# Writing the first PEER head's gates into a zeroed DRAM matrix with plain indirect DMAs instead of adding indirect DMAs

## The reference, cut to what matters

```python
def peer(h, w_q, sub_keys, u_tab, v_tab):      # shortened
    q = (xc @ w_q).reshape(ch, PEER_HEADS, 2, half)
    s = jnp.einsum('thpd,hpnd->thpn', q, sub_keys)
    v1, i1 = lax.top_k(s[:, :, 0], PEER_TOPK)
    v2, i2 = lax.top_k(s[:, :, 1], PEER_TOPK)
    ...
    e = i1_picked * N_KEYS + i2_picked          # one of 128*128 experts
    g = jax.nn.softmax(vals, axis=-1)
    act = jax.nn.gelu(jnp.einsum('td,thkd->thk', xc, u_tab[e])) * g
    return jnp.einsum('thk,thkd->td', act, v_tab[e])
```

## Time and profile before

| what | us |
|---|---|
| median of 3 runs | 3285.22 |
| lowest, highest | 3275.11, 3285.28 |
| profiled execution, its span | 3278.9 |
| TensorE matmul busy | 3197.4 |
| VectorE busy | 2016.1 |
| GpSimd busy | 1912.5 |
| ScalarE busy | 1237.3 |

### The profile page before, as it was taken

One profiled execution on the slowest core, in us unless ns is written; L12 is line 12 of the kernel. 1 busy time (PEld: TensorE's weight loads), 2 busy tenths in 40 slices (PEclk: granted clock), 3 DMA queues, 4 the chain that ended last, 5 costly groups with the idle time before them and its releaser, 6 DMA issues. The chain is left out here.

```text
span 3278.9 us, 47570 instructions
## 1 busy us (share of the span) xinstructions
PE 3197.4 (98%) x15034; PEld 2600.4 (79%) x15034; DVE 2016.1 (61%) x4043; ACT 1237.3 (38%) x1838; POOL 1912.5 (58%) x1318
## 2 busy tenths in 40 slices
PE   8889999999999999999899899999999999999999
PEld 7578888888887788887766678888888887888887
DVE  4667575752224888888646656676732225888888
ACT  3544233334433333333425633333332223333333
POOL 0005888888888756555000007888888886655554
PEclk9999999999999999999999999999999999999999
DMA  5925565666667999999319115655566668999998
GB/s 191 337 74 133 119 149 117 133 148 144 144 146 232 370 350 348 352 345 333 124 34 320 41 65 127 139 135 128 125 145 145 145 145 274 355 351 351 355 347 303
DMA packets 399381, 681.95 MB, mean 208 GB/s; under 512 B 145472, under 2 KB 239680, under 8 KB 399040
## 3 DMA queue, kind: packets, MB, share of 16 engines
q1 hardware_dynamic: 218944, 520.95, 47.1%
q0 software_dynamic: 155648, 134.82, 20.1%
q10 hardware_dynamic: 24704, 25.17, 2.3%
HBM read 560.85 MB, written 119.94 MB: 208 GB/s over the span
## 5 line engine op out<-in xcount | busy, mean ns | idle before, releaser
L1783 POOL DMA_INDIRECT gate_matrix<-pe_misc x768 | 1285.8, 1674 | 734.9 <-DVE pe_misc L2354 501.5
L2052 PE MATMUL psum<-split,ex_ah 128*128 128x512 f32 x2976 | 921.7, 391 | 10.1 <-DVE ex_al L2497 8.1
L427 PE MATMUL psum<-up_hhi,up_hi 128*128 128x512 f32 x2048 | 798.1, 390 | 0.0
L427 PE MATMUL psum<-up_hlo,up_hi 128*128 128x512 f32 x2048 | 796.8, 389 | 0.0
L427 PE MATMUL psum<-up_hhi,up_lo 128*128 128x512 f32 x2048 | 796.8, 389 | 0.0
L418 DVE TENSOR_TENSOR up_lo<-up_raw,up_hi 128x1024 fp32r<-128x1024 f32 x256 | 313.7, 1226 | 757.9 <-ACT up_hi L414 693.6
L2052 PEld LDWEIGHTS psum<-split,ex_ah 128*128 128x128 f32 x2976 | 555.3, 188 | 139.7 <-DVE ex_al L2497 20.8
L2052 PE MATMUL psum<-split,ex_al 128*128 128x512 f32 x1488 | 579.2, 389 | 0.0
L1793 POOL DMA_INDIRECT ex_gv<-in_v,ga_at x256 | 274.0, 1070 | 329.2 <-DVE x_sb L2447 306.6
L427 PEld LDWEIGHTS psum<-up_hhi,up_lo 128*128 128x128 f32 x2048 | 384.4, 188 | 79.8
L427 PEld LDWEIGHTS psum<-up_hlo,up_hi 128*128 128x128 f32 x2048 | 384.5, 188 | 79.3
(11 more groups left out here) (374 smaller groups left out, 3164.6 us busy)
## 6 DMA issues: line engine op xcount, KB each, us to landing
up_raw<-in_uT SPq DMA_DIRECT2D x256, 512.0 KB
ro_wq<-in_v SPq DMA_DIRECT2D x256, 512.0 KB
gelu<-up_z SPq DMA_DIRECT2D x256, 256.0 KB
pe_misc<-gelu SPq DMA_DIRECT2D x256, 192.0 KB
ex_gm<-gate_matrix SPq DMA_DIRECT2D x124, 384.0 KB
gate_matrix<-ga_at ACTq DMA_DIRECT2D x8, 3072.0 KB, 13.6
gate_matrix<-ga_at SPq DMA_DIRECT2D x8, 3072.0 KB, 23.2
ro_wq<-in_peer_wq SPq DMA_DIRECT2D x32, 512.0 KB
```

What stands on the lines that cost most here:

```text
L427: last = pe.matmul(self.ps[:, a, :], w[:, a, dc, :], h[:, dc, :], start=(dc == 0 and m == 0), stop=(dc == DC - 1 and m == 2))
L1783: pool.indirect_dma_start(place, bass.IndirectOffsetOnAxis(ap=to[:, j:j + 1], axis=0), gates[:, j:j + 1], None, compute_op=ALU.add).then_i ...
L2052: last = pe.matmul(psy[:, o, :], w[:, par, a, toks], v[:, par, a, cols], start=False, stop=(final and m == 2))
```

## The change

The helper `scatter` gives each indirect DMA the operation to do at its destination. It was an addition for all heads. Now it is a plain write (bypass) for head 0 and an addition for heads 1 to 7.

```diff
@@ def scatter(self, pool, gmat, to, gates, h, t)
             pool.wait_ge(done.sem, done.base + 16 * TOPK * h)
         for j in range(h * HW + t * TOPK, h * HW + (t + 1) * TOPK):
             pool.indirect_dma_start(place, bass.IndirectOffsetOnAxis(ap=to[:, j:j + 1], axis=0), gates[:, j:j + 1], None,
-                                    compute_op=ALU.add).then_inc(done.sem, 16)
+                                    compute_op=ALU.add if h > 0 else ALU.bypass).then_inc(done.sem, 16)
```

## The result

| kernel | runs | median us | lowest to highest |
|---|---|---|---|
| before, beside it | 4 | 3281.64 | 3275.11 to 3285.28 |
| changed | 4 | 3365.65 | 3360.25 to 3368.66 |

The ratio is 1.0254, 95% interval 1.0237 to 1.0272. The forecast was 3284.5 us in a range that ended at 3293. The profiled execution has a span of 3361.8 us, 82.9 more than before, with the same 47570 instructions.

What follows compares the result with a forecast made beforehand. PE was taken to bound the kernel. Head 0's 2 x 29 us saved on POOL became waiting or ended unneeded, 0 to -1 us on PE; with the run-to-profile difference carried over, 3284.5 us, range 3272 to 3293.

Steps and rivals of the forecast that it cites:

- What bounds the kernel now: Whole kernel: PE bounds, busy 98% of the span; it loses only 0.34 and 1.12 us around the two change-overs.
- Part 1, POOL's time: Head 0's 48 scatters per layer: slot 1.4 us instead of 1.997, so POOL finishes head 0 29 us earlier.
- "wrong if": Failure signs: first 48 slots over 2.05 us, no POOL wait before the 49th, or change-over PE time moving over 2 us.
- "PE full in the U stretches": Sign expected in the changed trace: PE without holes during the U products, and the change-overs as before.
- Part 2, what is late next: Head 1's start: POOL waits for DVE's gates, so only 1.5 us are won per layer and 27 us become waiting.
- Part 3, the end: Change-overs after the last scatters: these end 1.5 us earlier in each layer, and PE gains zero.
- SP's wait at L1945: Layer 0's end, SP waiting for the last scatter's completion: about 1.9 instead of 3.4 us.
- Part 4, DMA load: DMA engines during head 0: cheaper plain writes for 96 of 768 scatters, where PE waits for nothing; worth 0.
- A (same price on POOL): Head 0's scatters: a plain write costs POOL the same as an add; 3285.2 us, chance 0.26.
- B (slower): Head 0: plain scatters held up beside DVE make POOL's end pass PE's slack; 3303 to 3405 us, chance 0.07.
- C (faster): Head 1's gates or change-overs: the 29 us reach PE, faster by more than 0.3%; chance 0.05.

Runs made afterwards that it cites:

- chip A: Chip of the first follow-up group; against the kernel before: head 1 plain 0.9990, all heads plain 0.9994, head 0 plain with pauses 1.0512.
- the paced kernel: Changed kernel (head 0 plain) with a GpSimd memset and drain after each head 0 scatter; 3448.62 us, 1.0512 of the kernel before.
- chips B to E: Chips of the four later follow-up groups; the unedited changed kernel against the kernel before: 1.0284, 1.0295, 1.0266 and 1.0284.
- with gathers: Head 0's 48 scatters of each layer replaced by plain 4-byte gathers from the same places; 3376.46 us, 1.0289 of the kernel before.
- chip C: Chip of the third group; against the kernel before: changed kernel 1.0295, head 1 plain 1.0273, all heads plain 1.2182, head 0 plain with pauses 1.0513.

## Why the prediction was wrong, step by step

**What bounds the kernel now**: right. PE does, without a hole; so whatever holds up PE is paid in full, and 82.1 of 82.9 us arise in head 0 (44.0 and 38.1).

**Part 1, POOL's time**: right in kind, and too dear. A slot of 1.4 us was forecast, 1.27 measured, since the plain scatter takes 0.97 us almost always (0.94 and stretching came to 1.1 in the forecast); in the mean of the 48 it is 1.33. POOL is done at 333.8 (forecast 337). None of the three "wrong if" came true: the slots were 1.33 us in the mean and not 2.05, the wait before the 49th was there (76.19 us, where 25 to 30 were forecast), and the change-overs kept their PE time. What went wrong lay outside that list; of the signs forecast, "PE full in the U stretches" is the one that failed. The Trainium skill, "SBUF — State Buffer", section "A bandwidth-pool intuition that's wrong (but worth ruling out)", with its 3100 ns beside VectorE, isn't borne out for these DMAs: with all 768 plain the longest took 2.08 us.

**Part 2, what is late next**: right about the mechanism and right about its size on chip A, where the 49th started at 365.35 (forecast 364.5). It failed on the sentence "DVE's time for head 1 isn't set by POOL: the selection is interleaved with the splits of U tiles, which keep PE's pace, and PE has no holes to give". Nothing on DVE or ACT waits for POOL indeed. But POOL's faster issue made the holes in PE, and through PE's late signals DVE's time for head 1 was set by POOL after all.

**Part 3, the end**: right; that an earlier end of the scatters is worth nothing is shown by POOL's 225.7 us of waiting in the all-plain kernel on chip A, at a ratio of 0.9994. SP's wait at L1945 was forecast at 1.9 us and stayed 3.4, since nothing became earlier.

**Part 4, DMA load**: this step failed. It weighed only the load of the DMA engines ("cheaper... PE waits for nothing... Worth 0") and was right on that: queue 0 moves 10752 packets fewer (144896), 112 for each plain scatter. What it never asked is what POOL's pace does to others. The mean slot fell from 2.00 to 1.33 us, and that term, costed at nothing, measured +83 us (84.0 by the medians). The long add had held GpSimd's issue to one DMA in 2.00 us, and that turned out to be a brake which nobody had put there as one.

**Rivals.** A (same price on POOL) is refuted by 0.97 us. B (slower) named the right sign with the wrong mechanism: it needs a head 0 that ends later on POOL, and head 0 ended 30 us earlier. Its arithmetic was confirmed by the paced kernel (170 against 169.0 us), so it would have been right about a slow scatter. C (faster) is refuted on chip A: even 201 us earlier scatters gain nothing. The rival that was missing is a fourth: a faster queue that slows the engine which bounds. With the trace of before it couldn't be priced. Its plain indirect DMAs beside a busy PE are the gathers: 49 unbroken from 1037.99 to 1115.02, but at 1.60 us in the mean, with PE busy for 74.71 of 77.00 us; at 1.26 us there are no more than nine in a row. That gap could have been named, and would have taken more than the 0.08 that I gave to slower.

**What stays open.** Two things. Why chip A loses nothing from what costs chips B to E 92 to 97 us isn't known, nor whether it is the chip or the time; the kernel before shows no difference among them. And what in the chip delays PE isn't settled: the runs show matmuls in the middle of a product 1.2 to 3.5 us apart, and signals 12 to 46 us behind the last matmul, both together, and nothing on the DMA side behind (a load that SP issued at 301.12 had moved its data by 304.5).

Three things in the traces narrow it. Where GpSimd stands idle after an unbroken run of 48, the signal that is latest comes 4 to 7 us after the last of them: at 338.2 after 333.8 in the changed kernel, at 337.8 after 331.9 with gathers, at 432.6 after 426.1 with head 1 plain. So PE's signal seems to be held for as long as the run goes on. Second, only PE is late: the signal of ACT's split (done at 299.84) starts DVE at 299.87, and that of DVE's (301.10) starts PE at 301.15. Third, instructions on their way through a DMA queue aren't what is missing. The queues that the profile calls instruction queues move nothing between 288 and 345 us of the changed kernel, and nothing between 375 and 560 us of all plain on chip C, where PE is busy for 133.49 of 185.00 us. It may still be how PE takes up its instructions, the path of PE's own signals, or the recording of events itself, since every run here was recorded; no kernel without recording was timed. On the last, the Trainium skill, "NOTIFIC — the notification-queue block", section "7.1 Overflow: three behaviours, one of which stalls the engine", says that the path that writes such records can, in one of its modes, hold up an engine when it fills. By that rule one would look for more records, but the instructions of the kernel are as many as before and the packets in head 0 fewer (24 a us instead of 72), so no run here supports it; none excludes it either.

## What to carry to other kernels

An operation that gets cheaper on a queue without a brake also comes faster: before changing GpSimd's indirect DMAs, work out the new slot, and if it falls well under what the trace has shown beside full PE stretches (2.00 us here in the mean; 1.74 and 1.77 did no harm, 1.43 did, and 1.49 hardly any with gathers beside the V products), treat the difference as an unpriced risk to the engine that bounds. If such DMAs must be plain, wait for landing after every fourth, which cost nothing here; but no version was faster than the kernel before, since the only gain was on an engine that nobody waited for. Measure such a change on more than one chip and more than once: by chip A alone it would have passed as harmless.

## What the runs showed of the hardware that was not expected

- Indirect DMAs issued by GpSimd mostly one in 1.20 to 1.30 us, 32 or 48 in a row, delay TensorE beside them: 44.0 and 38.1 us for 48 of them here, 89.5 us for each 96 with all plain on chip C. In runs of up to 16 (mean 1.43 us) they cost half; at 1.74 us on average, or in runs of 4 and 8 (1.77), nothing was lost. It struck on chips B to E and in the first comparison, and not on chip A.
- While this goes on, TensorE's signal that a product is finished comes late, by 46 us in the changed kernel and by 50 us with head 1 plain on chip C (product done at 382.6, signal at 432.6).
- It makes no difference whether they write or read (1.0289 with gathers, 1.0266 with writes on the same chip), and little how many elements they carry (1.0226 with 64, 1.0284 with 128).
- A plain 4-byte scatter to 128 places holds GpSimd for 0.97 us, one to 64 places for 0.90, and an adding one to 128 for 1.55: half the places save 0.07 us, the plain write saves 0.58.
- On the same chain the signals of ScalarE and VectorE came at once (299.84 to 299.87, 301.10 to 301.15). The Trainium skill, "SBUF — State Buffer", section "Who interferes with whom", says that PE and ACT never wait on anyone. That speaks of memory ports, and the traces don't contradict it there; but it can't be read as saying that PE is out of reach of what GpSimd issues, by 23.21 busy us of 60.
